# Earlier norm transposes, later retention transposes, and direct products in the first two pairs of each Up pass of a hybrid decoder block

## What is computed

```python
h = rms_norm(x, attn_norm_g)
z = h @ w_in                       # split in qa,ka,va (attention), qr,kr,vr,gr (retention), up (pooling)
ya = sliding_window_attention(...) # 6 query heads, 2 key/value heads, window 128, sinks, relative bias
yr = retention(qr, kr, vr, gr)     # chunks of 128: inner scores, running state R, per-head norm, silu gate
yp = pool_mixer(up, pool_w, pool_scale)
x  = x + concat(ya, yr, yp) @ w_out
h  = rms_norm(x, mlp_norm_g)
x  = x + square(relu(h @ w_up)) @ w_down      # w_up 1024 x 4096, w_down 4096 x 1024
return rms_norm(x, final_norm_g)
```

## Time and profile before

| | us |
|---|---|
| median of 3 runs (lowest, highest) | 2162.47 (2158.6, 2165.51) |
| the profiled execution, its span | 2158.43, 2156.2 |
| PE busy | 2053.3 (95%) |
| DVE busy | 1354.5 (63%) |
| ACT busy | 922.8 (43%) |
| POOL busy | 478.2 (22%) |
| mean granted clock of TensorE | 0.983 |

### The profile page before, as it was taken

One profiled execution on the slowest core, in us unless ns is written; L12 is line 12 of the kernel. 1 busy time (PEld: TensorE's weight loads), 2 busy tenths in 40 slices (PEclk: granted clock), 3 DMA queues, 4 the chain that ended last, 5 costly groups with the idle time before them and its releaser, 6 DMA issues.

```text
span 2156.2 us, 28165 instructions
## 1 busy us (share of the span) xinstructions
PE 2053.3 (95%) x10172; PEld 1723.9 (80%) x10172; DVE 1354.5 (63%) x1864; ACT 922.8 (43%) x1565; POOL 478.2 (22%) x387
## 2 busy tenths in 40 slices
PE   8998999899989998699999799999999999999998
PEld 6987798779878977478888578888778888888887
DVE  3347344734563366877777877777666757767666
ACT  4443343334334433544555545444443334433333
POOL 6256435553654363300000300000000000000001
PEclk9999999999999999899999899999999999999999
DMA  7122422242224113166777355577885666955562
GB/s 269 62 88 92 159 69 69 98 155 68 69 103 157 59 69 127 44 160 159 172 163 175 100 144 150 147 186 208 258 319 212 256 243 269 361 217 230 230 269 93
DMA packets 101957, 349.14 MB, mean 162 GB/s; under 512 B 10395, under 2 KB 12220, under 8 KB 84412
## 3 DMA queue, kind: packets, MB, share of 16 engines
q1 hardware_dynamic: 97212, 330.54, 47.5%
q10 hardware_dynamic: 4608, 16.78, 2.0%
HBM read 270.61 MB, written 76.68 MB: 161 GB/s over the span
## 4 chain that ended last, share of the span: by engine, by line
PE 52%; DVE 2%; DMA 1%; issue 1%; ACT 0%; POOL 0%; SPq 0%; POOLq 0%; DVEq 0%; ACTq 0%
PE bank L1847 17%; PE bank L1849 17%; PE bank L1848 17%; DMA d_raw<-in_wdn 1%; DVE h_lo L1440 0%; POOL h_lo L818 0%; PE bank L2078 0%; DMA wraw<-in_wup 0%; DVE w_lo L1587 0%; DVE wt L1579 0%; SPq L620 0%; DVE wraw L1579 0%; ACT w_hi L1071 0%; ACT h_hi L1081 0%; DVE hraw L1435 0%
## 5 line engine op out<-in xcount | busy, mean ns | idle before, releaser
L1847 PE MATMUL bank<-h_hi,w_lo 128*128 128x512 f32 x896 | 354.4, 396 | 39.3 <-ACT tA L1098 17.7
L1847 PE MATMUL bank<-d_hi,u_lo 128*128 128x512 f32 x896 | 349.0, 390 | 4.0 <-DVE d_lo L1719 3.9
L1848 PE MATMUL bank<-h_lo,w_hi 128*128 128x512 f32 x896 | 352.3, 393 | 0.0
L1849 PE MATMUL bank<-h_hi,w_hi 128*128 128x512 f32 x896 | 352.1, 393 | 0.0
L1848 PE MATMUL bank<-d_lo,u_hi 128*128 128x512 f32 x896 | 348.6, 389 | 0.0
L1849 PE MATMUL bank<-d_hi,u_hi 128*128 128x512 f32 x896 | 348.6, 389 | 0.0
L688 POOL TENSOR_TENSOR ring_lo<-stage,ring_hi 128x1024 fp32r<-128x1024 f32 x104 | 246.8, 2394 | 283.6 <-ACT ring_hi L850 283.4
L1134 ACT ACTIVATE u_hi<-u_raw 128x1024 fp32r<-128x1024 f32 x112 | 118.5, 1058 | 333.9 <-PE bank L1849 318.8
L1719 DVE TENSOR_TENSOR u_lo<-u_raw,u_hi 128x1024 fp32r<-128x1024 f32 x112 | 137.1, 1224 | 179.5 <-ACT u_hi L1134 179.5
L1847 PE MATMUL bank<-ring_hi,hT_lo 128*128 128x384 f32 (+1 forms) x672 | 245.0, 365 | 0.3 <-DVE hT_lo L1394 0.2
L1849 PE MATMUL bank<-ring_hi,hT_hi 128*128 128x384 f32 (+1 forms) x672 | 235.9, 351 | 0.0
(11 more groups left out here) (187 smaller groups left out, 3451.0 us busy)
## 6 DMA issues: line engine op xcount, KB each, us to landing
u_raw<-u_dram SPq DMA_DIRECT2D x56, 1024.0 KB, 4.8
d_raw<-in_wdn SPq DMA_DIRECT2D x56, 1024.0 KB, 6.9
stage<-in_wmix SPq DMA_DIRECT2D x108, 512.0 KB, 3.3
u_dram<-ur SPq DMA_DIRECT2D x32, 1280.0 KB, 8.7
wraw<-in_wup SPq DMA_DIRECT2D x128, 256.0 KB, 2.9
e_raw<-in_wdn SPq DMA_DIRECT2D x24, 1024.0 KB, 8.9
xn<-in_x SPq DMA_DIRECT2D x16, 512.0 KB, 4.7
xq<-in_x ACTq DMA_DIRECT2D x16, 512.0 KB, 6.3
```

The lines of the kernel that those rows point to most:

```text
L1847: pe.matmul(dst, al, bh, start=(first and k == 0), stop=False, skip_group_check=chain)
L1848: pe.matmul(dst, ah, bl, start=False, stop=False, skip_group_check=chain)
L1849: last = pe.matmul(dst, ah, bh, start=False, stop=(final and k == n - 1), skip_group_check=chain)
```

## The change

1. The norm transposes of a quarter's next quarter move from the head of the quarter to between its last output tiles: block 0 behind tile 12, blocks 1 and 2 behind tile 13, block 3 behind tile 15. They use banks S0, S1, T1, OB. ACT's `x_hi` and DVE's `x_lo` move with them. Quarter 0's four blocks stand ahead of the loop; on ACT they stand ahead of the split of weight unit 0.
2. In every quarter `y_transposes` of blocks 0 to 3 moves behind one more output tile or step: block 0 behind tile 5, block 1 behind the rest of tile 8 and `ret_outs(2)`, block 2 behind tile 11, block 3 behind tile 13. `ret_outs(3)` moves from behind tile 10 to behind tile 11. DVE's steps are reordered to suit.
3. Pairs 0 and 1 of each pass (pairs 0, 1, 16, 17 of 32) are done directly: 8 products on the unsummed blocks, no `w_sum`, four weight operands instead of seven, results straight from the banks by ACT (`direct_out`), and four DVE additions (`direct_sums`) for the stored combinations. h's sums S1 to S4 and their low parts are made during these pairs. A21 needs operands of its own (role 7, in slot 6, which role 6 takes afterwards).
4. All low parts of h are made on DVE; POOL makes none. Pass 0's blocks of h are transposed one by one among tiles 12 to 15, and the last three among the first products. Pass 1's are transposed behind pairs 4 to 11 instead of 7 to 14.

The core of the diff:

```diff
-        XN_AT = (0, 4096, 8192, 180224, 184320)
+        XN_AT = (0, 4096, 8192, 196608, 217088)
-        H_FROM = (A11, A12, None, A22, A21, A12, A11)
-        HX_SLOT = (0, 1, 2, 3, 4, 2, 3, 4), (2, 2, 2, 2, 2, 2, 2, 2)
+        A21_ROLE = 7
+        H_FROM = (A11, A12, A21, A22, None, A12, A11, A21)
+        H_SLOT = (0, 1, 2, 3, 4, 5, 6, 6)
+        HX_SLOT = (0, 1, 2, 3, 4, 0, 1, 2), (2, 2, 2, 2, 2, 2, 2, 2)
+        def direct(n):
+            return n % NPAIR < 2
         def norm_bank(b, j):
-            return ((T0, T1), (S0, S1), (dense[1], dense[2]), (OB, T0))[b][j]
+            return ((S0, S1), (T1, OB))[b % 2][j]
...
@@ ScalarE
             def mixer_act(q, last):
-                for b in range(NB):
-                    x_hi(q, b)
                 split_hi(q, 1)
...
+                    square_x2(q, 1, last)
+                    x_hi(q, 0, True)
+                    yR_high(q, 3)
+                    x_hi(q, 1, True)
+                    x_hi(q, 2, True)
+                    square_x2(q, 2, last)
+                    x_hi(q, 3, True)
+                    square_x2(q, 3, last)
             for b in range(NB):
                 square_x(0, b)
+            for b in range(NB):
+                x_hi(0, b, False)
             split_hi(0, 0)
@@ VectorE, the mixer
                 yP_low(q, 0)
-                yR_low(q, 0)
                 rot_a(q, 2)
                 rot_add(q, 2)
                 evac_x2(q, 5)
+                yR_low(q, 0)
                 state(q, 1)
...
+                    x_lo(q, 0, True)
+                    evac_x2(q, 13)
+                    yR_low(q, 3)
+                    x_lo(q, 1, True)
+                    norm_ahead(q, 3, last)
+                    x_lo(q, 2, True)
+                    evac_x2(q, 14)
+                    evac_x2(q, 15)
+                    x_lo(q, 3, True)
@@ VectorE, the first two pairs of a pass
+                if n % NPAIR == 0:
+                    if p:
+                        combine_end(n - 1)
+                        h_low(p, A21_ROLE)
+                        for k in range(3):
+                            w_low(n + 1, k)
+                    else:
+                        for k in range(3):
+                            w_low(n + 1, k)
+                        sums(p, "S1")
+                    sums(p, "S2")
+                    sums(p, "S4")
+                    sums(p, "S3")
+                    h_low(p, 4)
+                    continue
@@ TensorE
             def mixer_pe(q, closing):
-                norm_transposes(q, 0)
-                norm_transposes(q, 1)
-                norm_transposes(q, 2)
-                norm_transposes(q, 3)
                 proj_first(q, 0)
...
                 pool_mix(q, 0)
+                out_tile(q, 5)
                 y_transposes(q, 0)
-                out_tile(q, 5)
                 ret_outs(q, 1)
...
                 ret_scores(q, 2)
-                y_transposes(q, 1)
                 out_tile_8_rest(q)
                 ret_outs(q, 2)
+                y_transposes(q, 1)
+                out_tile(q, 9)
                 qk_transposes(q, 3)
-                out_tile(q, 9)
+                out_tile(q, 10)
                 ret_scores(q, 3)
+                out_tile(q, 11)
                 y_transposes(q, 2)
-                out_tile(q, 10)
                 ret_outs(q, 3)
-                out_tile(q, 11)
                 out_tile(q, 12)
+                if closing:
+                    h_transposes(0, 0)
+                else:
+                    norm_transposes(q, 0, True)
+                out_tile(q, 13)
                 y_transposes(q, 3)
+                if closing:
+                    h_transposes(0, 1)
+                    h_transposes(0, 2)
+                else:
+                    norm_transposes(q, 1, True)
+                    norm_transposes(q, 2, True)
+                out_tile(q, 14)
+                if closing:
+                    h_transposes(0, 3)
+                    h_transposes(0, 4)
+                out_tile(q, 15)
+                if not closing:
+                    norm_transposes(q, 3, True)
...
+            def direct_product(n, k):
+                p, i = n // NPAIR, k // 2
+                w = (0, 1, 2, 3, 0, 1, 2, 3)[k]
+                h = (0, 1, 0, 1, 6, 3, 6, 3)[k]
...
-            h_transposes(0, 6)
-            h_transposes(0, 7)
+            h_transposes(0, 5)
             for n in range(PAIRS):
-                for k in range(NK):
-                    up_product(n, k)
-                if 7 <= n < 15:
-                    h_transposes(1, n - 7)
+                if direct(n):
+                    for k in range(8):
+                        direct_product(n, k)
+                        if n == 0 and k < 2:
+                            h_transposes(0, 6 + k)
+                else:
+                    for k in range(NK):
+                        up_product(n, k)
+                if 4 <= n < 12:
+                    h_transposes(1, n - 4)
```

More of the change, by code:

```diff
@@ new lines, in count, with product_at, w_sum_at, copy_at @@
+        def count(per_direct, per_pair, n, i):
+            return sum(per_direct if direct(m) else per_pair for m in range(n)) + i + 1
+        def product_at(n, k):
+            return count(8, NK, n, k)
+        def w_sum_at(n, i):
+            return count(0, 4, n, i)
+        def copy_at(n, i):
+            return count(0, 3, n, i)
+        def c_at(n, i):
+            return count(4, 10, n, i)
+        def r_at(n, i):
+            return count(8, 6, n, i)
+        def w_order(n):
+            return (0, 1, 2, 3) if direct(n) else (0, 1, 2, 4, 5, 3, 6) if n % NPAIR == 2 else (0, 1, 2, 3, 4, 5, 6)
@@ new lines, in h_sum, with h_low @@
+                    dve.tensor_tensor(v[:, A12, :], v[:, A12, :], v[:, A21, :], ALU.subtract).then_inc(h_sum_done, 1)
+            def h_low(p, k, blocks=range(TB)):
+                for b in blocks:
+                    dve.wait_ge(h_hi_done, h_hi_at(p, k, b))
+                    dve.tensor_tensor(h_lo[H_SLOT[k]][:, :, cols_of(b)], h_source(k, b).rearrange("p (c t) -> p c t", c=4),
+                                      h_hi[H_SLOT[k]][:, :, cols_of(b)].bitcast(F32), ALU.subtract).then_inc(h_sum_done, 1)
@@ L1453, in norm_ahead @@
                     x_norm(q, NB + b)
+                elif b == 0:
+                    h_norm(0, 0)
                 else:
+                    h_norm(0, 2 * b - 1)
                     h_norm(0, 2 * b)
-                    h_norm(0, 2 * b + 1)
-                if last and b == 3:
-                    h_sum(0, "S1", 0)
-                    h_sum(0, "S2", 0)
             def mixer_dve(q, last):
-                for b in range(NB):
-                    x_lo(q, b)
                 dve.wait_ge(o_done.sem, o_done.before(q, 3))
@@ L1555, in _ @@
             dve.wait_ge(s_relw, 2)
+            for b in range(NB):
+                x_lo(0, b, False)
             with dve.Fori(0, NQ - 1) as q:
@@ L1590, in combine @@
+                s = w_slot(n, k)
+                if not direct(n) and k in (2, 3, 4, 6):
+                    dve.wait_ge(w_sum_done, w_sum_at(n, {2: 1, 3: 3, 4: 0, 6: 2}[k]))
+                dve.tensor_tensor(w_lo[s][:, :, :].rearrange("p c n -> p (c n)"), w_source(n, k),
+                                  w_hi[s][:, :, :].rearrange("p c n -> p (c n)").bitcast(F32), ALU.subtract).then_inc(w_lo_done, 1)
             def combine(n, i):
+                last = before_direct(n)
                 if i == 0:
-                    dve.wait_ge(prod_done, NK * n + 2)
@@ L1637, in sums @@
                     h_sum(p, name, b)
[L1639 to L1642 removed]
+            h_low(0, 0, range(3, TB))
             w_low(0, 0)
+            h_norm(0, 5)
+            h_low(0, 1, range(0, 2))
             w_low(0, 1)
[L1645 to L1648 removed]
+            h_norm(0, 6)
+            h_low(0, 1, range(2, TB))
@@ L1649, in _ @@
             w_low(0, 2)
[L1650 to L1651 removed]
+            h_norm(0, 7)
             w_low(0, 3)
[L1653 to L1666 removed]
```

650 lines of the change are left out of this document (360 added, 290 removed).

## The result

The changed kernel takes **2125.89 us** (median of 4 runs, 2123.12 to 2126.89), the kernel before 2163.56 (4 runs, 2158.60 to 2165.51): ratio 0.9839, 95% interval 0.9824 to 0.9853. 2127 was forecast. The profiled execution took 2126.89 us, 31.5 less than that of before (2158.4); the medians lie 37.7 apart, and the ratio puts the gain at 34.8.

What follows compares the result with a forecast made beforehand. PE, busy 95% of the span, was taken as the bound, with gains only where it waits. Terms -5.1 + 7.4 - 2.3 + 19.9 + 15.4 = 35.3 us off 2162.5 gave 2127 us; 8-in-10 range 2109 to 2147.

Steps and rivals of the forecast that it cites:

- The passes of Up: Up's two pass starts, with direct pairs: gains of 19.9 us in pass 0 and 15.4 us in pass 1.
- Rival (c): Pass starts: h operands arrive as late as now, the whole loss stays, four products come on top; 2173 us, chance 0.06.
- (a): Pass starts: stalls go only half, DVE or ACT late by one operand several times; 2145 us, chance 0.25 with (d).
- (d): Direct pairs: `direct_out` frees banks late, each pass loses some 6 us; 2139 us, chance 0.25 together with (a).
- Rival (b): More gain: loop edge overlapped (+5), kernel start at lower bound (+2.2), retention's waits gone (+8); 2112 us, chance 0.13.
- One sign: Direct pairs: the forecast is wrong if pairs 0, 1, 16 or 17 take over 24 us each.
- The kernel start: Start to first projection: weight unit 0 split behind all eight `x_hi`, costing 5.1 us.
- The steps: Between quarters: moved transposes shorten the three steps to 21.9 us before waits for unit 1; gain 7.4 us, bounds 2.4 to 12.4.
- The wait for unit 1: Projection 1 behind the loop's edge waits 2.5 us for weight unit 1 in the two looped steps, none in the third.
- The retention transposes: Moved `y_transposes` in four quarters: a loss of 2.3 us, bounds -5 to +10.
- The step that block 1's wait only changes its name: Rest of tile 8 still waits for `yP_low(1)`: the 3.3 us are renamed, and three transposes cost 0.35 us.

Runs made afterwards that it cites:

- Four_products: The changed kernel with the second product of pairs 4 to 7 run twice, four products more: 2138.91 us, ratio 0.9904 to the kernel before.
- Dve_alone: The kernel before, with low parts of h operands 1, 3 and 6 on DVE instead of POOL, no direct pair: 2151.54 us, ratio 0.9963.
- pool_low: The changed kernel with low parts of h operands 1, 3 and 6 of both passes back on POOL: 2130.52 us, ratio 0.9862.
- early_split: The changed kernel with ACT splitting weight unit 0 ahead of the first quarter's eight `x_hi`, as before the change: 2118.38 us, ratio 0.9809.
- unit1_ahead: The changed kernel with weight unit 1 of the next quarter split ahead of the loop's edge, quarter 0's ahead of the loop: 2126.42 us, ratio 0.9836.

## Why the prediction was right, and where its terms were off

**The passes of Up (35.3 written, 35.5 found).** Both sums held, 19.7 for 19.9 and 15.8 for 15.4, with their new waits where they were placed: 3.18 for `hx` where 3.4 was written, 0.85 for 1.1, the first product at the low clock, 0.55 for the 0.9 of the chain copy. Four_products shows the price of four extra products at a place without waits. Dve_alone and pool_low divide the gain: 8 us come by taking POOL's low parts away alone, and putting them back beside the direct pairs costs 5; the other 27 come with the direct pairs. They are not shown to be theirs alone in pass 0: there 7.0 of the 19.7 us lie ahead of the first product (29.4 us from tile 12's end to it before, 22.4 after), where the norms, the transposes, the buffers of h and DVE's order changed with them, and no run has one without the other. In pass 1 the earlier transposes are not what helps: ACT's first high part of h stands 6.3 us behind pair 15's start before (1192.68 - 1186.34) and 6.2 after (1176.73 - 1170.50). Rival (c) is out by the time line, and in pool_low, where part of DVE's instructions in pair 0 took 1.4 to 1.7 us beside POOL, that pair lost 1.7 us. Rivals (a) and (d) are out by the time line too, in which no operand or bank of a direct pair is late behind `h_transposes(0,7)`. Rival (b) is out as well: the edge is not hidden, the start is 4.65 us late, and the retention's waits have new names. One sign was written wrong: a direct pair of over 24 us was to refute the forecast, and pair 0 took 26.7, which is what the prediction's own terms for it give (21.8 of products, 1.8 of transposes, 1.1 and 1.9: 26.6).

**The kernel start** came out -4.65 for -5.1, its cause shown by early_split. What the step lacked is the clock: the first projection's matmuls are slow, which adds 1.8 us (139.5 for 137.7 from there to output tile 3).

**The steps.** Without the waits for unit 1 they took 20.0, 20.1 and 19.1 us from tile 12's start, where 21.9 less tile 11's 3.4, 18.5, was written: the loop's edge shows 0.64 to 0.77 us on PE too, and `pt` of block 3 came 1.1 late for 0.6. The wait for unit 1 was 1.7 and 1.5 for 2.5, and the stretch to output tile 3 grew only by 0.6 and 1.1, since in the kernel before 3.4 us of a low clock fell into projection 0 of both quarters, which cost some 1.5 and is gone:

```profile
232.00:235.40 3.40, 3.40 (x18) 3.40 (x18) 3.40 (x5) 3.28 (x4) 1.92 (x1) 0.50 0.86 287
```

(From the kernel before. Behind the busy times of the engines stands the granted clock, 0.50; it is 0.50 too from 443.70 to 447.00, in quarter 2's.) No term had this. The errors nearly cancel: 8.4 - 1.7 = 6.7 for 7.4, so the closeness of this term is in part luck. The wait stands behind ACT's loop edge (2.96 us in the changed kernel, 2.52 written), and unit1_ahead, which splits the unit ahead of the edge, takes it away.

**The retention transposes** are the term that was mis-sized, -2.3 for -4.0, inside its bound of -5. Every quarter of both kernels has a low clock at the long wait of tile 8. Where it lasts 3.4 us, tile 3 to tile 12 takes 48.1 to 48.2 us after (quarters 1 to 3) and 47.3 to 47.7 before (quarters 0 and 3). In quarter 3 block 0 costs 1.3 (0.7 written: `ret_outs(1)` waits 1.15 for `decay_scores(1)`, and the `qk` transposes 1.87, 2.0 in the other quarters, for `yR_low(0)` behind `rot_add` and evacuation 5), block 1 0.2 (0.35), and block 2 gives 0.6 (0.62): 0.8 in all. So the moves by themselves cost some 2.6 us over the four quarters (48.15 less 47.5, four times), near the 2.3 written. The rest of the term is longer slow clock, which no step had: 4.5 us in quarter 0 after, less 2.1 and 0.9 in quarters 1 and 2 before. The step that block 1's wait only changes its name was right as far as it went. But it took `yP_low(1)`'s place behind `ret_y(1)` as given, and that place had its reason only as long as PE needed `ret_y(1)` first. There lay 17 us, more than the +10 that bounds this term.

**The size against the profile.** Profile to profile the gain was 31.5, by medians 37.7, and 35.3 was written. The four runs of the kernel before that give 2163.56 lie high: its medians beside the experiments, which ran on several chips, were 2157.32 to 2161.45, against which 2125.89 is 31 to 36 less. So the gain is known to a few us only, and 35.3 is right within that.

## What to carry to other kernels

When work of the waiting engine is moved behind other work, look at once at the queue of the engine that feeds it: its order was made for the old sequence. Block 1's transposes and DVE's order gave 2126 (transposes moved), 2108 (both), 2131 (DVE's order alone) and 2118 us (neither, with block 0's transposes back too, worth 3.6 by the trace; ratios 0.9839, 0.9758, 0.9873, 0.9797): a local optimum that neither edit leaves by itself. And where a stage starts with all of its operands late, work that asks for fewer of them can pay even at the price of extra matmuls on the bounding engine: with 10.9 us of products more, the two starts got 35.5 us shorter, of which 8 come without these products.
